# A gelu branch turned round: tokens in partitions, gelu out of PSUM, the result transposed by the matrix engine

## The chip, the cores and the metric

The kernel runs on one core of a Trainium2 chip. The metric is the device time in microseconds of one execution. All data are float32; the large products are computed in split form (below) as float32r matmuls.

## What is computed

Two residual blocks over 256 tokens of width 2048. The change lies in the recurrent branch of the first one:

```
proj = rmsnorm(x) @ w_in                         # xr, yr, q, k, v, g_rnn, g_attn
xr   = rg_lru(causal_conv(xr), ...)              # gates: two block-diagonal products, sigmoid;
                                                 # a = exp(..), h[t] = a[t] h[t-1] + b[t]
y_rnn = xr * gelu(yr)                            # the gelu branch: 2048 features
mix  = sigmoid(g_rnn) * (y_rnn @ w_rnn_proj) + sigmoid(g_attn) * (y_att @ w_attn_proj)
```

An MLP, and then a second block (differential attention and a state-space branch), follow and are not touched.

## The kernel before

**Units.** Every large product is cut into units of 512 output columns with 2048 rows of weights: 16 k tiles, taken in 8 subgroups of two. For a subgroup SyncE loads 512 KB into one of four slots of `raw`; ScalarE rounds them to float32r (`split_hi`, L674, `w_hi`), VectorE subtracts (`split_lo`, L1187, `w_lo`); the matrix engine computes three products, hi*hi, hi*lo and lo*hi. `split_hi` of a subgroup waits until the matrix engine has finished the subgroup four before it (`pe_used`), and the two splitting engines work three subgroups ahead (`LEAD`). Units alternate between the accumulators `acc[0]` and `acc[1]` (two PSUM banks each); `acc_free` tells that one has been read.

**Two forms.** A *token* unit has the activations as the stationary operand (128 tokens) and 512 columns of weights streaming: 2 x 3 matmuls of 512 columns per k tile, 96 in a unit; tokens come out in partitions. A *feature* unit (`by_feature=True`) has 128x128 blocks of weights stationary and 256 tokens streaming: 4 x 3 matmuls of 256 columns per k tile, 192 in a unit; features come out in partitions, as the recurrence along the tokens needs them.

**Order.** Each engine's order is written out by hand: `unit(...)` on the matrix engine and `steps(...)` on ScalarE and VectorE take tables of hooks, called after a given k tile or subgroup. The stage in question: after four pairs of q and xr units (with the attention beside them) come the four units of the gelu branch (U_YR + c, c = 0 to 3), all feature units, then the mix units (token units). The first unit of the branch has the last heads' attention beside it. Beside unit U_YR + c + 1 (for c = 3 beside the first mix unit) runs the recurrence of the 512 features of chunk c:

- the matrix engine, after k tile 1: `rg(c)`, 32 float32 matmuls (L2138); the first gate goes into `tps` (two banks), the second into `sides` (two banks)
- ScalarE: step 0 `gelu(c)` (L865), step 1 `gates(c)` (tanh out of `tps` and `sides`, L838 and L841), step 2 `decays(c)` (L851, L855), step 4 `root(c)` (L860), step 7 `y_high(c)` (L829)
- VectorE: step 3 `decay(c)` (L1451 to L1453), step 5 `states(c)` with the four scans (L1459 to L1466), step 6 `y_product(c)` (L1472), step 7 `y_low(c)` (L1477). For c = 3 the scans are at step 6, the product at step 7 and `y_low` in the next unit.

Each step begins with a split, and the hooks come after it. When a gelu unit is complete, VectorE multiplies it by the row of 1/rms (`L1491`) out of the accumulator into `k_t` or `stg`, in turn; ScalarE puts the gelu over it in place.

Names: `stg`, `tmp`, `tmp2`, `k_t` are 128x1024 buffers in SBUF; `rec4` is `tmp`, `a4` is `tmp2` (the profile may show both as `tmp`), `r4` and `i4` lie in `slab_g` (shown as `slab_dg_f`). `rstd` holds 1/rms of a token by partition, `row` the same along the free dimension. `y_ready` counts two per chunk: scans, product.

Of the kernel before, what the change touches and what calls it, by code (L numbers as in the profile page):

```python
# [16 lines left out]
P = 128  # L17
# [78 lines left out]
def griffin_block_then_ssm_block(nc, a, inv_freq, out):  # L96
    with ExitStack() as ctx:
# [12 lines left out]
        def sem(name):  # L110
            return ctx.enter_context(nc.semaphore(name))
# [98 lines left out]
        conv_ready, rg_done, w_ready = sem("conv_ready"), sem("rg_done"), sem("w_ready")  # L210
        xc_read, tap_ready = sem("xc_read"), sem("tap_ready")
        d_ready, root_ready, y_ready = sem("d_ready"), sem("root_ready"), sem("y_ready")
        y_hi_ready, gelu_ready = sem("y_hi_ready"), sem("gelu_ready")

        z_ready, tanh_ready, zs_ready = sem("z_ready"), sem("tanh_ready"), sem("zs_ready")

# [139 lines left out]
        r4, i4 = slab_g[:, 8:12, :], slab_g[:, 12:16, :]  # L356
        xc4 = stg[:, :, :].rearrange("p t (k c) -> p (t k) c", c=SEQ)
        xr_c = i4
        yr_c = [k_t[:, :, :], xc4]
        turned4 = xc4  # L360
        rec4 = tmp[:, :, :].rearrange("p t (k c) -> p (t k) c", c=SEQ)
        a4 = tmp2[:, :, :].rearrange("p t (k c) -> p (t k) c", c=SEQ)
# [252 lines left out]
        def tok(bank):  # L615
            return bank[:, :].rearrange("p (t n) -> p t n", t=TT)

        def feat(bank):
            return bank[:, :].rearrange("p (k c) -> p k c", c=SEQ)
# [42 lines left out]
        def _(act):  # L662
# [168 lines left out]
            def gates(c):  # L831
                act.wait_ge(rg_done, c + 1)
                if c:
                    act.wait_ge(y_ready, 2 * c)
                else:
                    act.wait_ge(conv_ready, NH + 1)
                for m in range(QPC):
                    nc.scalar.activation(r4[:, m, :], tps[:, m * SEQ:(m + 1) * SEQ], ACT.Tanh, scale=0.5,  # L838
                                         bias=half_b[:, c * QPC + m:c * QPC + m + 1])
                for m in range(QPC):  # L840
                    ins = nc.scalar.activation(i4[:, m, :], side[m // 2][:, m % 2 * SEQ:(m % 2 + 1) * SEQ], ACT.Tanh,  # L841
                                               scale=0.5, bias=half_b[:, KT + c * QPC + m:KT + c * QPC + m + 1])
                chain.mark(ins)

            def decays(c):

                chain.wait()
                act.wait_ge(lam_ready, 1)
                for m in range(QPC):
                    s2 = lru[:, 6, c * QPC + m:c * QPC + m + 1]  # L850
                    ins = nc.scalar.activation(rec4[:, m, :], r4[:, m, :], ACT.Exp, scale=s2, bias=s2)  # L851
                chain.link(ins)
                for m in range(QPC):
                    s2 = lru[:, 7, c * QPC + m:c * QPC + m + 1]
                    ins = nc.scalar.activation(r4[:, m, :], r4[:, m, :], ACT.Tanh, scale=s2, bias=s2)  # L855
                ins.then_inc(w_ready, 1)
# [4 lines left out]

            def gelu(c):
                u = U_YR + c
                act.wait_ge(acc_free[u % 2], u // 2 + 1)
                nc.scalar.activation(yr_c[c % 2], yr_c[c % 2], ACT.Gelu_apprx_tanh).then_inc(gelu_ready, 1)  # L865

            def beside_recurrence(c):
                places = {0: [lambda: gelu(c)], 1: [lambda: gates(c)], 2: [lambda: decays(c)], 4: [lambda: root(c)]}
# [312 lines left out]
        def _(dve):  # L1181
# [16 lines left out]
            def unit_over(i, stride, const):  # L1198
                dve.wait_ge(pe_used, lin(i, stride, const + S))
# [267 lines left out]
                ins.then_inc(y_ready, 1)  # L1467

            def y_product(c):
                dve.wait_ge(gelu_ready, c + 1)  # L1470
                dve.wait_ge(y_ready, 2 * c + 1)
                V.tensor_tensor(a4, yr_c[c % 2], rec4, ALU.mult).then_inc(y_ready, 1)  # L1472

            def y_low(c):
                at = slice(c * QPC, (c + 1) * QPC)
# [8 lines left out]
            for c in range(NH):  # L1484
                u = U_YR + c
                steps(None, 0, u * S, beside_recurrence(c - 1) if c else beside_yr)
                if c == 0:
                    dve.wait_ge(tps_free, T_QX + NH)
                unit_over(None, 0, u * S)
                rows_ = row[:, :].unsqueeze(1).broadcast_to([P, QPC, SEQ])  # L1490
                V.tensor_tensor(yr_c[c % 2], feat(acc[u % 2]), rows_, ALU.mult).then_inc(acc_free[u % 2], 1)  # L1491


            def mix_unit(i, c, n, hooks=None):
# [456 lines left out]
        def _(pe):  # L1951
            T = nc.tensor

            def unit(i, g_stride, g0, u_stride, u, hi, lo, by_feature=False, hooks=None, before=None, k_tiles=KT,
                     halves=False):


                par = u % 2
                hooks, before = hooks or {}, before or {}
                if i is not None or u >= 2:  # L1960
                    pe.wait_ge(acc_free[par], lin(i, u_stride // 2, u // 2))
                for s in range(k_tiles // 2):
                    for f in before.get(s, []):
                        f()
                    pe.wait_ge(lo_ready, lin(i, g_stride, g0 + s + 1))
                    if halves and s == k_tiles // 2 - 1:

                        for t in range(TT):
                            o = acc[par][:, t * NC:(t + 1) * NC]
                            c = slice(t * P, (t + 1) * P)  # L1970
                            for e in range(2):
                                wh, wl = w_hi[:, s % RING, e, :], w_lo[:, s % RING, e, :]
                                T.matmul(o, hi[:, 2 * s + e, c], wh, start=False, stop=False)
                                T.matmul(o, hi[:, 2 * s + e, c], wl, start=False, stop=False)
                                ins = T.matmul(o, lo[:, 2 * s + e, c], wh, start=False, stop=e == 1)
                            ins.then_inc((acc_half, pe_used)[t], 1)
                        break
                    for e in range(2):
                        k = 2 * s + e
                        first, last = k == 0, k == k_tiles - 1  # L1980
                        wh, wl = w_hi[:, s % RING, e, :], w_lo[:, s % RING, e, :]
                        if by_feature:
                            for m in range(QPC):
                                o = acc[par][:, m * SEQ:(m + 1) * SEQ]
                                c = slice(m * P, (m + 1) * P)

                                T.matmul(o, wh[:, c], hi[:, k, :], start=first and m % 2 == 0, stop=False,  # L1987
                                         skip_group_check=True)
                                T.matmul(o, wh[:, c], lo[:, k, :], start=False, stop=False, skip_group_check=True)  # L1989
                                ins = T.matmul(o, wl[:, c], hi[:, k, :], start=False, stop=last, skip_group_check=True)  # L1990
                        else:
                            for t in range(TT):
                                o = acc[par][:, t * NC:(t + 1) * NC]
                                c = slice(t * P, (t + 1) * P)
                                T.matmul(o, hi[:, k, c], wh, start=first, stop=False)  # L1995
                                T.matmul(o, hi[:, k, c], wl, start=False, stop=False)  # L1996
                                ins = T.matmul(o, lo[:, k, c], wh, start=False, stop=last)  # L1997
                        if e == 1:
                            ins.then_inc(pe_used, 1)
                        for f in hooks.get(k, []):  # L2000
                            f()
# [124 lines left out]
            def rg(c):  # L2126
                pe.wait_ge(conv_ready, c + 2)
                pe.wait_ge(rgw_landed[c % 2], 64 * (c // 2 + 1))
                if c:
                    pe.wait_ge(w_ready, c)  # L2130
                else:
                    pe.wait_ge(att_out, 4 * NH)
                for g in range(2):
                    for b in range(2):
                        bank = tps[:, b * NC:(b + 1) * NC] if g == 0 else side[b][:, :]
                        for m in range(2):
                            for k in range(2):
                                ins = T.matmul(bank[:, m * SEQ:(m + 1) * SEQ],  # L2138
                                               rgw[c % 2][g][:, 2 * b + k, m * P:(m + 1) * P], slab_d[:, c * QPC + 2 * b + k, :],
                                               start=k == 0, stop=k == 1)  # L2140
                ins.then_inc(rg_done, 1)

            for c in range(NH):
                unit(None, 0, (U_YR + c) * S, 0, U_YR + c, h_hi, h_lo, by_feature=True,
                     hooks={1: [lambda: rg(c - 1)]} if c else beside_yr)

            def mix_unit(i, c, n, hooks=None):
                hi, lo = ((h_hi, h_lo), (slab_er, slab_ir), (h_hi, h_lo), (slab_fr, slab_hr))[n]
                u = U_MIX + 4 * c + n
                unit(i, 4 * S, u * S, 4, u, hi, lo, hooks=hooks)  # L2150

            mix_unit(None, 0, 0, {1: [lambda: rg(NH - 1)]})
            for c in range(NH - 1):
                for n in (1, 2, 3):
                    mix_unit(None, c, n)
# [197 lines left out]
```

## Time and profile before

| | |
|---|---|
| median of 3 runs | 2240.53 us (2240.46 to 2240.6) |
| profiled execution, its time | 2240.62 us |
| its span, first to last instruction | 2238.9 us |
| matrix engine (PE) busy | 2227.7 us, 99% |
| VectorE (DVE), ScalarE (ACT), GpSimd (POOL) busy | 70%, 54%, 12% |
| mean granted clock of the matrix engine | 1.000 |

The span and what lies around it make up the execution's time (1.7 us more). Matmuls overlap in the pipeline, so the busy share is that of a queue that is never empty and not of a peak rate; the distance from one start to the next is what a matmul costs. PEld are the weight loads. Idle time of an engine stands in brackets, with what ended it.

### The profile page before, as it was taken

The numbers are of one execution on the slowest core, as the hardware profiler recorded it, in microseconds if no ns is written. First come the engines' busy times: TensorE is split into PE (matmuls) and PEld (weight loads), VectorE is DVE, ScalarE is ACT, GpSimd is POOL, SyncE is SP. The second block draws the span as 40 slices with busy tenths as digits, with TensorE's granted clock in tenths as the row PEclk, the third lists the DMA queues.
The fourth block names the chain that finished last, engine by engine and source line by source line (L and its number), as shares of the span: only waits on it lengthen the run. The fifth ranks groups of instructions, "written<-read, shape, count | busy, mean of one in ns | idle before, by whom it ended". The sixth has DMA issues, their size and how long they took to land.

```text
span 2238.9 us, 32782 instructions
## 1 busy us (share of the span) xinstructions
PE 2227.7 (99%) x11645; PEld 1875.1 (84%) x11645; DVE 1575.0 (70%) x2081; ACT 1218.3 (54%) x1915; POOL 275.1 (12%) x319
## 2 busy tenths in 40 slices
PE   9999999999999999999999999999999999999999
PEld 7888999888888888888888888889987788888887
DVE  6666657664664778757857856966999967766774
ACT  6666667544444456555655656555444446554443
POOL 2132220000000102211212121120000001110000
PEclk9999999999999999999999999999999999999999
DMA  8555454666666856666666666665666655555665
GB/s 242 153 170 150 144 186 142 191 194 194 193 189 197 255 189 213 206 208 190 219 206 193 215 209 204 192 219 177 185 185 206 194 179 168 168 161 177 199 200 167
DMA packets 215350, 427.09 MB, mean 191 GB/s; under 512 B 14097, under 2 KB 14385, under 8 KB 214961
## 3 DMA queue, kind: packets, MB, share of 16 engines
q1 hardware_dynamic: 206960, 398.57, 57.3%
q0 software_dynamic: 8048, 26.62, 3.9%
q8 instruction: 91, 1.49, 0.3%
q14 instruction: 43, 0.34, 0.0%
q10 hardware_dynamic: 208, 0.07, 0.0%
HBM read 414.71 MB, written 10.49 MB: 190 GB/s over the span
## 4 chain that ended last, share of the span: by engine, by line
PE 93%; DVE 3%; ACT 2%; issue 1%; DMA 0%; POOL 0%; DVEq 0%; ACTq 0%
PE acc L1995 26%; PE acc L1997 26%; PE acc L1996 26%; PE acc L1987 4%; PE acc L1989 3%; PE acc L1990 3%; PE sides L2213 1%; PE tps L2223 1%; PE sides L2087 1%; PE tps L2105 1%; DVE w_lo L1187 1%; ACT w_hi L674 1%; PE tps L2098 0%; ACT tmp L851 0%; DVE tmp L1466 0%
## 5 line engine op out<-in xcount | busy, mean ns | idle before, releaser
L1187 DVE TENSOR_TENSOR w_lo<-raw,w_hi 128x1024 fp32r<-128x1024 f32 x752 | 927.4, 1243 | 574.1 <-ACT w_hi L674 568.7
L674 ACT ACTIVATE w_hi<-raw 128x1024 fp32r<-128x1024 f32 x752 | 790.3, 1058 | 729.1 <-PE acc L1997 598.1
L1995 PE MATMUL acc<-w_hi,h_hi 128*128 128x512 f32 x1440 | 569.5, 395 | 2.7 <-DVE w_lo L1187 1.8
L1997 PE MATMUL acc<-w_hi,h_lo 128*128 128x512 f32 x1440 | 561.1, 390 | 0.0
L1996 PE MATMUL acc<-w_lo,h_hi 128*128 128x512 f32 x1440 | 560.7, 389 | 0.0
L1995 PEld LDWEIGHTS acc<-w_hi,h_hi 128*128 128x128 f32 x1440 | 270.4, 188 | 69.4 <-issue 15.1
L1997 PEld LDWEIGHTS acc<-w_hi,h_lo 128*128 128x128 f32 x1440 | 270.3, 188 | 57.2
L1996 PEld LDWEIGHTS acc<-w_lo,h_hi 128*128 128x128 f32 x1440 | 270.6, 188 | 53.3
L1995 PE MATMUL acc<-w_hi,slab_dg_r 128*128 128x512 f32 x756 | 294.1, 389 | 0.0
L1996 PE MATMUL acc<-w_lo,slab_dg_r 128*128 128x512 f32 x756 | 294.1, 389 | 0.0
L1997 PE MATMUL acc<-w_hi,slab_dg_r 128*128 128x512 f32 x756 | 294.1, 389 | 0.0
L1987 PE MATMUL acc<-h_hi,w_hi 128*128 128x256 f32 x768 | 221.3, 288 | 0.8 <-issue 0.8
L1989 PE MATMUL acc<-h_lo,w_hi 128*128 128x256 f32 x768 | 217.2, 283 | 0.0
L1990 PE MATMUL acc<-h_hi,w_lo 128*128 128x256 f32 x768 | 217.1, 283 | 0.0
L1211 DVE STREAM_TRANSPOSE stg<-tmp 32x256 f32<-32x256 f32 x384 | 167.3, 436 | 5.8
L1997 PEld LDWEIGHTS acc<-w_hi,slab_dg_r 128*128 128x128 f32 x756 | 141.9, 188 | 29.5
L1996 PEld LDWEIGHTS acc<-w_lo,slab_dg_r 128*128 128x128 f32 x756 | 141.9, 188 | 29.4
L1995 PEld LDWEIGHTS acc<-w_hi,slab_dg_r 128*128 128x128 f32 x756 | 141.9, 188 | 29.4
L1987 PEld LDWEIGHTS acc<-h_hi,w_hi 128*128 128x128 f32 x768 | 146.8, 191 | 7.1 <-issue 6.9
L1989 PEld LDWEIGHTS acc<-h_lo,w_hi 128*128 128x128 f32 x768 | 147.0, 191 | 0.2
L1990 PEld LDWEIGHTS acc<-h_hi,w_lo 128*128 128x128 f32 x768 | 146.9, 191 | 0.0
L1995 PE MATMUL acc<-w_hi,slab_f_r 128*128 128x512 f32 x256 | 100.4, 392 | 0.0
(390 smaller groups left out, 2320.4 us busy)
## 6 DMA issues: line engine op xcount, KB each, us to landing
raw<-in_w_in_dram SPq DMA_DIRECT2D x328, 512.0 KB, 4.0
raw<-in_w_mlp_up_dram SPq DMA_DIRECT2D x128, 512.0 KB, 4.2
raw<-in_w_mlp_down_dram SPq DMA_DIRECT2D x128, 512.0 KB, 4.4
raw<-in_w_out_dram SPq DMA_DIRECT2D x64, 512.0 KB, 4.4
raw<-in_w_rnn_proj_dram SPq DMA_DIRECT2D x32, 512.0 KB, 4.0
raw<-in_w_attn_proj_dram SPq DMA_DIRECT2D x32, 512.0 KB, 4.1
trig_scratch<-tmp POOLq DMA_DIRECT2D x32, 256.0 KB, 4.8
raw<-in_w_proj_ssm_dram SPq DMA_DIRECT2D x16, 512.0 KB, 3.8
```

The costliest lines, as they stand in the source:

```text
L674: nc.scalar.activation(w_hi[:, j % RING], raw[:, j % RING], ACT.Copy).then_inc(hi_ready, 1)
L1187: V.tensor_tensor(w_lo[:, j % RING], raw[:, j % RING], w_hi[:, j % RING].bitcast(F32), ALU.subtract)\
L1211: ins = V.transpose(dst, src)
L1987: T.matmul(o, wh[:, c], hi[:, k, :], start=first and m % 2 == 0, stop=False, skip_group_check=True)
L1989: T.matmul(o, wh[:, c], lo[:, k, :], start=False, stop=False, skip_group_check=True)
L1990: ins = T.matmul(o, wl[:, c], hi[:, k, :], start=False, stop=last, skip_group_check=True)
L1995: T.matmul(o, hi[:, k, c], wh, start=first, stop=False)
L1996: T.matmul(o, hi[:, k, c], wl, start=False, stop=False)
L1997: ins = T.matmul(o, lo[:, k, c], wh, start=False, stop=last)
L2087: ins = T.matmul(side[n][:, t * P:t * P + (t + 1) * P], q_c[at, p, t * P:(t + 1) * P], k_c[at, 0:(t + 1) * P], start=True, stop=True)
L2105: ins = T.matmul(y_banks[64 * n:64 * n + 64, t, :], v_c[:, s, :], prob_t[p % 2][:, n, b * P:(b + 1) * P], start=s == 0, stop=s == t)
L2213: ins = T.matmul(side[j % 2][:, part * SEQ:(part + 1) * SEQ], b_t[at, part, :], u_feat[at, n // 4, :], start=True, stop=True)
```

## The change

The four units of the gelu branch become token units. When one is complete, ScalarE takes the gelu directly out of the accumulator, with 1/rms as the scale per partition, in two activations of 128x512 into `stg`. VectorE's multiplication goes. The matrix engine then turns the eight 128x128 blocks of `stg` into `tps`, after k tile 7 of the next unit (`turn_yr`), once `gates` has read both gates there; the product takes its operand from `tps`. The next `rg` writes `tps` too, so it now waits for that product (`y_ready` at 2c) and for `gates_read`, where it waited for `w_ready`. Two semaphores take the place of `gelu_ready` and of a link of ScalarE's chain.

```diff
--- before.py
+++ after.py
@@ -210,7 +210,8 @@
         conv_ready, rg_done, w_ready = sem("conv_ready"), sem("rg_done"), sem("w_ready")
         xc_read, tap_ready = sem("xc_read"), sem("tap_ready")
         d_ready, root_ready, y_ready = sem("d_ready"), sem("root_ready"), sem("y_ready")
-        y_hi_ready, gelu_ready = sem("y_hi_ready"), sem("gelu_ready")
+        y_hi_ready = sem("y_hi_ready")
+        gates_read, yr_turned = sem("gates_read"), sem("yr_turned")
 
         z_ready, tanh_ready, zs_ready = sem("z_ready"), sem("tanh_ready"), sem("zs_ready")
 
@@ -356,7 +357,6 @@
         r4, i4 = slab_g[:, 8:12, :], slab_g[:, 12:16, :]
         xc4 = stg[:, :, :].rearrange("p t (k c) -> p (t k) c", c=SEQ)
         xr_c = i4
-        yr_c = [k_t[:, :, :], xc4]
         turned4 = xc4
         rec4 = tmp[:, :, :].rearrange("p t (k c) -> p (t k) c", c=SEQ)
         a4 = tmp2[:, :, :].rearrange("p t (k c) -> p (t k) c", c=SEQ)
@@ -840,11 +840,11 @@
                 for m in range(QPC):
                     ins = nc.scalar.activation(i4[:, m, :], side[m // 2][:, m % 2 * SEQ:(m % 2 + 1) * SEQ], ACT.Tanh,
                                                scale=0.5, bias=half_b[:, KT + c * QPC + m:KT + c * QPC + m + 1])
-                chain.mark(ins)
+                ins.then_inc(gates_read, 1)
 
             def decays(c):
 
-                chain.wait()
+                act.wait_ge(gates_read, c + 1)
                 act.wait_ge(lam_ready, 1)
                 for m in range(QPC):
                     s2 = lru[:, 6, c * QPC + m:c * QPC + m + 1]
@@ -861,8 +861,14 @@
 
             def gelu(c):
                 u = U_YR + c
-                act.wait_ge(acc_free[u % 2], u // 2 + 1)
-                nc.scalar.activation(yr_c[c % 2], yr_c[c % 2], ACT.Gelu_apprx_tanh).then_inc(gelu_ready, 1)
+                unit_over(None, 0, u * S)
+                if c:
+                    act.wait_ge(yr_turned, c)
+                else:
+                    act.wait_ge(tps_ready, T_QX + NH)
+                for t in range(TT):
+                    ins = nc.scalar.activation(stg[:, t, :], tok(acc[u % 2])[:, t, :], ACT.Gelu_apprx_tanh, scale=rstd[:, t:t + 1])
+                ins.then_inc(acc_free[u % 2], 1)
 
             def beside_recurrence(c):
                 places = {0: [lambda: gelu(c)], 1: [lambda: gates(c)], 2: [lambda: decays(c)], 4: [lambda: root(c)]}
@@ -1467,9 +1473,9 @@
                 ins.then_inc(y_ready, 1)
 
             def y_product(c):
-                dve.wait_ge(gelu_ready, c + 1)
+                dve.wait_ge(yr_turned, c + 1)
                 dve.wait_ge(y_ready, 2 * c + 1)
-                V.tensor_tensor(a4, yr_c[c % 2], rec4, ALU.mult).then_inc(y_ready, 1)
+                V.tensor_tensor(a4, feat(tps), rec4, ALU.mult).then_inc(y_ready, 1)
 
             def y_low(c):
                 at = slice(c * QPC, (c + 1) * QPC)
@@ -1484,11 +1490,6 @@
             for c in range(NH):
                 u = U_YR + c
                 steps(None, 0, u * S, beside_recurrence(c - 1) if c else beside_yr)
-                if c == 0:
-                    dve.wait_ge(tps_free, T_QX + NH)
-                unit_over(None, 0, u * S)
-                rows_ = row[:, :].unsqueeze(1).broadcast_to([P, QPC, SEQ])
-                V.tensor_tensor(yr_c[c % 2], feat(acc[u % 2]), rows_, ALU.mult).then_inc(acc_free[u % 2], 1)
 
 
             def mix_unit(i, c, n, hooks=None):
@@ -2127,7 +2128,8 @@
                 pe.wait_ge(conv_ready, c + 2)
                 pe.wait_ge(rgw_landed[c % 2], 64 * (c // 2 + 1))
                 if c:
-                    pe.wait_ge(w_ready, c)
+                    pe.wait_ge(gates_read, c)
+                    pe.wait_ge(y_ready, 2 * c)
                 else:
                     pe.wait_ge(att_out, 4 * NH)
                 for g in range(2):
@@ -2140,16 +2142,26 @@
                                                start=k == 0, stop=k == 1)
                 ins.then_inc(rg_done, 1)
 
+            def turn_yr(c):
+                u = U_YR + c
+                pe.wait_ge(acc_free[u % 2], u // 2 + 1)
+                pe.wait_ge(gates_read, c + 1)
+                for t in range(TT):
+                    for b in range(QPC):
+                        ins = T.transpose(tps[:, b * SEQ + t * P:b * SEQ + (t + 1) * P], stg[:, t, b * P:(b + 1) * P],
+                                          ident[:, :])
+                ins.then_inc(yr_turned, 1)
+
             for c in range(NH):
-                unit(None, 0, (U_YR + c) * S, 0, U_YR + c, h_hi, h_lo, by_feature=True,
-                     hooks={1: [lambda: rg(c - 1)]} if c else beside_yr)
+                unit(None, 0, (U_YR + c) * S, 0, U_YR + c, h_hi, h_lo,
+                     hooks={1: [lambda: rg(c - 1)], 7: [lambda: turn_yr(c - 1)]} if c else beside_yr)
 
             def mix_unit(i, c, n, hooks=None):
                 hi, lo = ((h_hi, h_lo), (slab_er, slab_ir), (h_hi, h_lo), (slab_fr, slab_hr))[n]
                 u = U_MIX + 4 * c + n
                 unit(i, 4 * S, u * S, 4, u, hi, lo, hooks=hooks)
 
-            mix_unit(None, 0, 0, {1: [lambda: rg(NH - 1)]})
+            mix_unit(None, 0, 0, {1: [lambda: rg(NH - 1)], 7: [lambda: turn_yr(NH - 1)]})
             for c in range(NH - 1):
                 for n in (1, 2, 3):
                     mix_unit(None, c, n)
```

## Rows read from the trace of the kernel before

**Rows 1.** The page: engines, busy us, share, instructions; granted clock in tenths
```profile
PE 2227.7 (99%) x11645; PEld 1875.1 (84%) x11645; DVE 1575.0 (70%) x2081; ACT 1218.3 (54%) x1915; POOL 275.1 (12%) x319
...
PEclk9999999999999999999999999999999999999999
```

**Rows 2.** Waits of PE over the span: total us, times, longest us
```profile
PE acc L1995 <- DVE w_lo L1187: 1.8, 2, 1.2
```

**Rows 3.** The chain of waits, 170 to 480 us: start us, us, what
```profile
296.02 1.57 ACT slab_dg_f L838 x4
...
400.92 1.15 DVE w_lo L1187
402.11 0.50 PE acc L1995
```

**Rows 4.** Timeline of PE and PEld, gate matmuls: start us, us, instruction
```profile
288.80 0.74 PEld L2138 LDWEIGHTS tps<-slab_dg_f 128*128 128x128 f32 x4
...
295.63 0.47 PE L1987 MATMUL acc<-h_hi,w_hi 128*128 128x256 f32 x1
...
318.74 0.31 PEld L2138 LDWEIGHTS tps<-slab_dg_f,slab_e_f 128*128 128x128 f32 x2
...
348.68 0.31 PEld L2138 LDWEIGHTS tps<-slab_dg_f 128*128 128x128 f32 x2
...
378.38 0.19 PEld L2138 LDWEIGHTS tps<-slab_dg_f,slab_e_f 128*128 128x128 f32 x1
```

**Rows 5.** Timeline of ACT and DVE in the first round
```profile
305.43 1.99 ACT L674 ACTIVATE w_hi<-raw 128x1024 fp32r<-128x1024 f32 x2
...
306.51 1.23 DVE L1187 TENSOR_TENSOR w_lo<-raw,w_hi 128x1024 fp32r<-128x1024 f32 x1 [5.23 <-ACT w_hi L674]
...
313.32 1.22 DVE L1459 SCALAR_TENSOR_TENSOR slab_dg_f<-tmp,slab_dg_f 128x1024 f32<-128x1024 f32 x1
...
319.31 1.22 DVE L1472 TENSOR_TENSOR tmp<-k_t,tmp 128x1024 f32<-128x1024 f32 x1
```

**Rows 6.** Timeline of DVE, the product of the third round
```profile
379.19 1.22 DVE L1472 TENSOR_TENSOR tmp<-k_t,tmp 128x1024 f32<-128x1024 f32 x1
```

**Rows 7.** Timeline of PE, first matmuls of units
```profile
200.43 0.50 PE L1995 MATMUL acc<-w_hi,h_hi 128*128 128x512 f32 x1
...
228.61 0.28 PE L1987 MATMUL acc<-h_hi,w_hi 128*128 128x256 f32 x1
...
256.98 0.38 PE L1987 MATMUL acc<-h_hi,w_hi 128*128 128x256 f32 x1
...
286.03 0.28 PE L1987 MATMUL acc<-h_hi,w_hi 128*128 128x256 f32 x1
...
404.99 0.39 PE L1995 MATMUL acc<-w_hi,slab_e_r 128*128 128x512 f32 x1
...
426.81 0.39 PE L1995 MATMUL acc<-w_hi,h_hi 128*128 128x512 f32 x1
```

**Rows 8.** Timeline of PE, eight transposes inside a token unit
```profile
49.91 1.03 PE L2010 MATMUL tps<-ident,stg 128*128 128x128 f32 x8
50.70 0.48 PE L1995 MATMUL acc<-w_hi,h_hi 128*128 128x512 f32 x1
51.01 0.40 PE L1996 MATMUL acc<-w_lo,h_hi 128*128 128x512 f32 x1
```

**Rows 9.** Timeline of PE, the matmul before the wait at 402 us
```profile
401.61 0.39 PE L1997 MATMUL acc<-w_hi,h_lo 128*128 128x512 f32 x1
```

**Rows 10.** ACT by line, 400 to 470 us; timeline of ACT and DVE
```profile
L894 ACT ACTIVATE tmp<-acc,small 128x512 f32<-128x512 f32 x4 | 2.5, 684 | 1.8 <-PE acc L1997 1.7
...
322.79 1.22 DVE L1491 TENSOR_TENSOR stg<-acc,t_low 128x1024 f32<-128x1024 f32 x1
...
324.05 1.06 ACT L865 ACTIVATE stg<-stg 128x1024 f32<-128x1024 f32 x1 [0.18 <-DVE stg L1491]
...
325.96 1.57 ACT L838 ACTIVATE slab_dg_f<-tps,half_b 128x256 f32<-128x256 f32 x4
```

## The prediction, made before the changed kernel was run

> **What bounds the kernel now.** I read the page first: the matrix engine is busy 99% of the span at the full granted clock (2.4 GHz) in all forty slices [rows 1]. Next the matrix engine's own waits: the longest single one is 1.2 us, and waits for VectorE's `w_lo` come to 1.8 us in all [rows 2]. So a microsecond added to or removed from the matrix engine's queue in this stage moves the end by a microsecond, unless another engine is late there. The chain of waits warns of just that: from the end of the first gate matmuls at 296 us to 402 us it runs through ScalarE and VectorE [rows 3], although the matrix engine waits for neither until the last 0.3 us. Something there must be nearly late, and I looked for it in the timeline.
>
> The loop is this. In each unit after the first of the branch, the matrix engine does one pair of k tiles (a subgroup), then the 32 float32 gate matmuls (L2138), then the other seven subgroups. The gate results go through `gates`, `decays`, `decay`, `root`, `states`, `scans` and end in `y_product`, all placed among the weight splits in the fixed orders of ScalarE and VectorE. The first weight load of the gate matmuls starts at 288.80, 318.74, 348.68 and 378.38 [rows 4]: intervals of 29.94, 29.94 and 29.70, in sum 89.58 us. The product of the first round starts at 319.31 and lasts 1.22: it ends at 320.53, which is **31.73 us after its gate matmuls began** [rows 4, 5]. In round three it is 379.19 + 1.22 - 348.68 = 31.73 again [rows 6]. The product thus ends 1.8 us after the next gate matmuls have begun. Before the change this harms nobody: it reads `k_t` or `stg` and `tmp`, no bank.
>
> **The new wait, the largest term.** After the change `y_product` reads the gelu from `tps`, and `rg(c)` writes `tps` again. So `rg` waits for `y_ready` at 2c, the end of the product of the round before. That end comes 31.73 us after its own round's start, and the queue is in order: everything behind `rg(c)` on the matrix engine stands still. Is the chain to the product paced by the matrix engine, so that it would shrink or stretch with it? The rows say no [rows 3, 5]. `gates` starts at 296.02 when the gate matmuls end, then come a split, `decays`, two splits from 305.43, VectorE's `w_lo` from 306.51, three steps of `decay`, two `w_lo`, `states` from 313.32, `scans`, a `w_lo`, and the product at 319.31. Each begins within a fraction of a microsecond of the one before it (the table loads of ScalarE fill the rest). Those splits that wait for the matrix engine (the tightest is the one between `gates` and `decays`, which wants two subgroups done) find it done at the same point of the round as now, or earlier: one token subgroup takes 2.72 us where a feature subgroup takes 2.88 (both below). I take 31.73 as it is.
>
> Without the wait the matrix engine would be back at `rg` after: gate matmuls 6.83 (288.80 to 295.63, [rows 4]); 84 matmuls of the seven subgroups; the eight transposes; 12 matmuls of the next first subgroup. An undisturbed token unit goes from 404.99 to 426.81, 21.82 us for 96 matmuls [rows 7], 0.227 each. So 84 are 19.1, plus 0.2 for the change of data type; 12 are 2.7. The transposes: 49.91 to 50.70 is 0.79 for the same eight blocks from `stg` to `tps`, and the first matmul behind it holds the next one up until 51.01, 0.31 where 0.23 is usual: 0.87 in all [rows 8]. Sum 29.7. The product ends at 31.73: a stall of 2.0 to 2.1 us.
>
> A start after a wait: VectorE's split at 400.92 ends at 402.07, the matrix engine starts at 402.11 [rows 3], so 0.04; and the first matmul there is put at 0.50 against 0.39 [rows 3, 9], since its weight load is not hidden. I take 0.04 + 0.08, between nothing and 0.3 as the bounds. A round is then 31.85. Three rounds are held (`rg(1)`, `rg(2)`, `rg(3)`): 3 x 31.85 = 95.55 against 89.58, **+6.0 us** (bounds: 5.6 with nothing, 6.5 with 0.3 each).
>
> **The first unit of the branch** has attention beside it. The same hooks ran beside a token unit from 200.43 to 228.61, 28.18 us; the feature unit took 256.98 to 286.03, 29.05 us [rows 7]. Saved 0.87, and 0.16 on the first subgroup of the next unit, before `rg(0)`: **-1.0**. The saving of the other three units (192 matmuls at 0.120, 23.1 us from 295.63 to 318.74 [rows 4], against 21.8: 1.3 each) goes into the stall and is in the 31.85 already. So do the three sets of transposes.
>
> What has the Trainium skill on this? The row shows 0.120 us a matmul of 256 columns and 0.227 of 512, a saving of 1.3 us a unit. "TensorE: Matmul & The Clock Gate", section "Back-to-back issue gap", gives N/2.4 + 2.5 ns, so by it, as an estimate, 109 and 216 ns and only 0.24 us a unit; it speaks against half of what turning the operands round could win. By that figure the first unit saves 0.2, not 0.9, and the sum would be 0.8 higher. The rows decide.
>
> **After `rg(3)`.** The fourth turn stands in the first mix unit, in nobody's shadow: +0.87. In exchange the wait for `w_lo` there goes (the matmul before it began at 401.61, so the next was due at 401.84 and began at 402.11, [rows 3, 9]): the matrix engine, 0.87 later, finds it ready; 0.27 of pause and 0.11 of restart are saved, 0.38. Together **+0.5**. The product of round three and `tanh` behind it keep their distance from `rg(3)`; the matrix engine comes 0.5 later to them, so nothing new is late.
>
> **What costs nothing.** `L1491` (1.22 us of VectorE, four times [rows 10]) goes. It stands after the product, and VectorE's next splits are for subgroups that the matrix engine wants only after 6.8 us of gate matmuls. The gelu becomes two activations from the bank, by the nearest row 684 ns each for one of 1.06 us: 0.3 us more on ScalarE. After the product ScalarE does `y_high`, a split, the table load, the gelu, a split, and then `gates`: the second round's `gates` begins at 325.96, 5.4 us after the product's end, a wait of 0.18 for L1491 included [rows 10]. With 0.3 more that is 5.7, while the gate matmuls will end 7 us after the product. Cover 1.3 us; if it were gone each microsecond would lengthen the round by one. `turn_yr` waits for the gelu and `gates_read`: `gates` is done 10.2 us after the round starts, the turn comes at 15. The product's other operand in a bank: L1491 read a bank and took 1.22 as well. `acc_free` comes from ScalarE about when it came from VectorE, and the bank is wanted a unit later. No transfer is issued or moved.
>
> **Sum.** -1.0 + 6.0 + 0.5 = +5.4 us on the profiled execution's 2240.62, hence 2246.0; its time is 0.1 above the median of the runs, which changes nothing that I can forecast. Behind the first mix unit all is bound by the matrix engine, so nothing is given back.
>
> **Rivals.**
> *The product is in time (not slower).* If the round's chain were under 29.7 us, no stall: -1.0 in the first part, 3 x (-1.3 + 0.87) = -1.3, +0.5 after: -1.8, 2238.8. For it: VectorE is without L1491. Against: L1491 is behind the product, not ahead of it, and both rounds show 31.73. It decides from 2.0 us off the chain. A chain shorter by 1 us leaves 2243.
> *The round grows.* The longer stall lets ScalarE's queue slip into `gates`: if the gelu cost the table load twice (1.28) or the split before it were late, rounds of 33: 3 x 33 - 89.6 = +9.4, and 2249.5. Against: 1.3 us of cover.
> *The clock falls in the stall.* A pause of 2 us is longer than any in the profile (1.2). At 1.2 GHz the gate matmuls after it take 6.8 more: +20, 2266. Against: the pauses at the start left the granted clock full [rows 1]. The same page of the Trainium skill, section Part 1, "The HAM clock gate", has the throttled state as the default that activity lifts; here no row shows it.
> *Faster.* It would take no stall and transposes at nothing: -1.0 - 3.9 - 0.4 = -5.3, 2235.3. The transposes take 0.79 in the queue wherever they stand.
>
> **Numbers.** Stall as worked out 0.70 (its own range 2245.0 to 2247.3), in time 0.10, shorter chain with part of the stall 0.08, grown round 0.08, clock 0.02, faster 0.02. A change under 0.2% (4.5 us, up to 2245.0) can't be told from none. Slower: 0.70 less the part of it that may fall short, plus 0.10, 0.75; faster 0.02; same 0.23. The range from 2242.0 to 2248.5 leaves out the case without a stall and most of the grown rounds.
>
> **What would show it.** Matrix engine idle about 2 us ahead of the gate matmuls three times, released by VectorE's product; gate matmuls 31.8 us apart; no idle ahead of the fourth turn; nothing waiting at 402; from the second mix unit on the old pattern, 5.4 later. Wrong if the product ends sooner than 31.5 after its gate matmuls, or if `gates` starts late.

## The result and the profile after

The changed kernel takes **2250.86 us** (median of 6 runs, 2248.79 to 2252.55) against 2240.49 us for the kernel before (6 runs): ratio 1.0046, 95% interval 1.0036 to 1.0056. It is slower, as forecast, but by 10.4 us where 5.4 were forecast, and outside the stated range (up to 2248.5). Its runs also spread over 3.8 us, those of before over 1.0.

The page of the changed kernel, engines and granted clock, beside [rows 1]:

```profile
span 2248.9 us, 32088 instructions
## 1 busy us (share of the span) xinstructions
PE 2231.7 (99%) x11293; PEld 1860.7 (83%) x11293; DVE 1569.6 (70%) x2077; ACT 1219.7 (54%) x1919; POOL 274.9 (12%) x319
...
PEclk9999999999999999999999999999999999999999
```

It shows next to nothing: the matrix engine is busy 99% as before, and the clock reads 9 in every slice. The only hint is the mean granted clock that goes with the run, 0.998 for 1.000; over a span of 2249 us, 0.002 short is 4 to 5 us. Five of the six runs have 0.998 and the slowest has 0.997. The waits of the matrix engine have a new first row, beside [rows 2]:

```profile
PE tps L2140 <- DVE tmp L1478: 6.0, 3, 2.0
```

L2140 are the gate matmuls, L1478 is the product: three pauses of 2.0 us. The timeline of the weight loads there, beside [rows 4]; the four starts are 31.94, 33.50 and 31.82 us apart where they were 29.94, 29.94 and 29.70:

```profile
286.93 0.19 PEld L2140 LDWEIGHTS tps<-slab_dg_f 128*128 128x128 f32 x1
...
318.87 0.30 PEld L2140 LDWEIGHTS tps<-slab_dg_f,slab_e_f 128*128 128x128 f32 x2 [2.40 <-issue]
...
352.37 0.30 PEld L2140 LDWEIGHTS tps<-slab_dg_f 128*128 128x128 f32 x2 [2.35 <-issue]
...
384.19 0.30 PEld L2140 LDWEIGHTS tps<-slab_dg_f,slab_e_f 128*128 128x128 f32 x2 [2.39 <-issue]
```

One interval is 1.6 us longer than its neighbours, though the pause ahead of it is no longer. The matmuls tell why:

```profile
302.24 1.03 PE L2151 MATMUL tps<-ident,stg 128*128 128x128 f32 x8
303.03 0.48 PE L1996 MATMUL acc<-w_hi,h_hi 128*128 128x512 f32 x1
...
318.90 5.38 PE L2140 MATMUL tps<-slab_dg_f,slab_e_f 128*128 128x256 f32 x16 [2.00 <-DVE tmp L1478]
...
352.40 3.69 PE L2140 MATMUL tps<-slab_dg_f 128*128 128x256 f32 x16 [1.96 <-DVE tmp L1478]
...
384.22 5.38 PE L2140 MATMUL tps<-slab_dg_f,slab_e_f 128*128 128x256 f32 x16 [2.00 <-DVE tmp L1478]
```

The same 16 matmuls take 3.69 us in one round and 5.38 in the two others. The stretches (window and its length in us, then busy time and instructions of each engine, then the granted clock as a share of 2.4 GHz, DMA):

```profile
316.70:318.90 2.20, 0.20 (x2) 0.03 (x1) 2.20 (x3) 0.12 (x1) 0.00 (x0) 1.00 0.07 11
...
320.30:323.70 3.40, 3.40 (x10) 2.65 (x9) 1.94 (x2) 3.37 (x5) 0.00 (x0) 0.50 0.78 227
...
350.40:352.40 2.00, 0.04 (x2) 0.03 (x1) 2.00 (x3) 0.12 (x1) 0.00 (x0) 1.00 0.03 9
352.40:359.20 6.80, 6.80 (x33) 6.00 (x33) 4.56 (x4) 5.38 (x6) 0.00 (x0) 1.00 0.77 228
...
385.10:388.50 3.40, 3.40 (x10) 2.73 (x9) 2.46 (x3) 3.37 (x5) 0.00 (x0) 0.50 0.83 264
832.30:835.70 3.40, 3.40 (x9) 2.62 (x9) 2.81 (x6) 2.08 (x5) 0.00 (x0) 0.50 0.00 0
```

Behind two of the three pauses the clock stands at 0.50, 1.2 GHz, for 3.4 us, and the matrix engine does half the work in them: 1.7 us lost each time. A third such stretch is at 832 us, where the turning of x for the MLP (transposes of the normalised x on the matrix engine) makes two pauses of 0.67 and 0.77 us. The first of the two is longer than in the kernel before:

```profile
821.79 1.36 PE L2032 MATMUL tps<-ident,slab_i_f 128*128 128x128 f32 x8 [0.30 <-DVE slab_i_f L1613]
...
829.99 1.36 PE L2033 MATMUL tps<-ident,slab_i_f 128*128 128x128 f32 x8 [0.67 <-DVE slab_i_f L1614]
```

(the first line from the kernel before, the second from the changed one). Forty slices of 56 us hide all three falls.

So the books of the profiled execution (2250.59 against 2240.62, +9.97) are: the first unit and all ahead of `rg(0)` 286.93 - 288.80 = -1.9, of which 0.7 is a start of the program that was 0.7 us quicker; the three rounds (384.19 - 286.93) - 89.58 = +7.7; from `rg(3)` to the second mix unit 28.69 for 26.61, +2.1; behind it +2.1, of which 1.7 is the fall at 832 and 0.37 the longer pause there. Three falls make 5.1 of the 10.0.

### The profile page after: what moved, and what is told of

Its sections match the earlier page's. It is cut to its first block, busy times and chain, and to the rows that moved or that the text cites. A ratio compares the mean times of both kernels' runs of the same rounds, so it can differ in the third digit from the quotient of the medians.

```text
span 2248.9 us, 32088 instructions
## 1 busy us (share of the span) xinstructions
PE 2231.7 (99%) x11293; PEld 1860.7 (83%) x11293; DVE 1569.6 (70%) x2077; ACT 1219.7 (54%) x1919; POOL 274.9 (12%) x319
## 4 chain that ended last, share of the span: by engine, by line
PE 95%; DVE 2%; ACT 2%; issue 1%; DMA 0%; POOL 0%; DVEq 0%; ACTq 0%
PE acc L1996 27%; PE acc L1998 26%; PE acc L1997 26%; PE acc L1988 3%; PE acc L1990 3%; PE acc L1991 3%; PE tps L2140 1%; PE sides L2225 1%; PE tps L2235 1%; PE sides L2140 1%; PE sides L2088 1%; PE tps L2106 1%; PE tps L2099 0%; ACT w_hi L674 0%; DVE w_lo L1193 0%
## 5 line engine op out<-in xcount | busy, mean ns | idle before, releaser
L1996 PE MATMUL acc<-w_hi,h_hi 128*128 128x512 f32 x1568 | 621.6, 396 | 2.0 <-DVE w_lo L1193 1.2
L1998 PE MATMUL acc<-w_hi,h_lo 128*128 128x512 f32 x1568 | 611.8, 390 | 0.0
L1997 PE MATMUL acc<-w_lo,h_hi 128*128 128x512 f32 x1568 | 611.3, 390 | 0.0
L1996 PEld LDWEIGHTS acc<-w_hi,h_hi 128*128 128x128 f32 x1568 | 294.8, 188 | 74.0 <-issue 15.6
L1988 PE MATMUL acc<-h_hi,w_hi 128*128 128x256 f32 x512 | 147.5, 288 | 0.8 <-issue 0.8
L1990 PE MATMUL acc<-h_lo,w_hi 128*128 128x256 f32 x512 | 144.8, 283 | 0.0
L1991 PE MATMUL acc<-h_hi,w_lo 128*128 128x256 f32 x512 | 144.7, 283 | 0.0
L1988 PEld LDWEIGHTS acc<-h_hi,w_hi 128*128 128x128 f32 x512 | 97.8, 191 | 5.9 <-issue 5.7
L1998 PE MATMUL acc<-w_hi,slab_h_r 128*128 128x512 f32 x256 | 99.7, 389 | 0.0
L1997 PE MATMUL acc<-w_lo,slab_f_r 128*128 128x512 f32 x256 | 99.6, 389 | 0.0
```

## The experiments

**Theory A:** the pause costs its length as forecast, and besides it lets the granted clock fall, which is the missing half. **Theory B:** the missing half comes from the new order itself (product from the bank, token units, later stages). **Theory C**, for the second set: pauses matter, but only among the changed kernel's instructions. Times are medians, each beside the kernel before on the same chip.

| kernel | us | before | ratio (95%) | pauses, us | low clock in the stage (profile) |
|---|---|---|---|---|---|
| changed | 2250.86 | 2240.49 | 1.0046 (1.0036 to 1.0056) | 2.00, 1.96, 2.00 | 2 of 3 |
| fill | 2246.14 | 2240.82 | 1.0026 (1.0016 to 1.0035) | none | none |
| fill_part | 2245.76 | 2241.08 | 1.0021 (1.0012 to 1.0031) | 1.36, 1.32, 1.31 | none |
| wait_alone | 2246.86 | 2240.82 | 1.0027 (1.0016 to 1.0038) | 1.66, 1.66, 1.79 | none |
| product_early | 2243.19 | 2240.82 | 1.0011 (1.0002 to 1.0020) | 1.09, 1.01, 1.08 | none |
| later_product | 2255.05 | 2241.08 | 1.0063 (1.0049 to 1.0077) | 3.14, 3.08, 3.11 | 3 of 3 |
| later_wait | 2256.37 | 2241.08 | 1.0068 (1.0054 to 1.0081) | 2.80, 2.79, 2.92 | 3 of 3 |
| copy_out | 2240.58 | 2240.82 | 0.9997 (0.9988 to 1.0006) | none | none |
| copy_and_warm | 2239.74 | 2241.08 | 0.9995 (0.9986 to 1.0004) | none | none |
| before_filled | 2240.85 | 2240.80 | 1.0000 (0.9991 to 1.0009) | none | none |
| copy_filled | 2239.82 | 2240.80 | 0.9996 (0.9987 to 1.0005) | none | none |

### fill: work in place of the pause

```diff
                 if c:
                     pe.wait_ge(gates_read, c)
+                    keep_turning(20)
                     pe.wait_ge(y_ready, 2 * c)
```

> The changed kernel with 20 transposes of the identity (into the second bank pair of the gates, which nobody reads any more) put ahead of the wait for the product, so that the matrix engine works through the pause instead of standing still. The three pauses stay as long, only filled. Theory A (the pause costs its own length, and twice a fall of the granted clock besides): the gate matmuls start 31.8 us apart all three times, the clock stays at 2.4 GHz in this stage, and the time is that of the forecast, 2245 to 2247. Theory B (the extra 5 us come from the new order itself: the operand in a bank, the token units, the later stages): nothing changes or it gets slower, 2249 to 2252.

2246.14, and the rounds are 31.9, 31.8 and 31.8 us. The stretches of fill around the three starts of the gate matmuls, at the full clock and without a gap:

```profile
318.00:330.00 12.00, 12.00 (x66) 10.64 (x65) 6.49 (x6) 8.43 (x15) 2.67 (x4) 1.00 0.63 184
350.00:362.00 12.00, 12.00 (x65) 10.58 (x64) 6.26 (x6) 8.65 (x15) 0.00 (x0) 1.00 0.63 177
382.00:394.00 12.00, 12.00 (x64) 10.54 (x63) 6.03 (x6) 8.83 (x15) 0.00 (x0) 1.00 0.59 176
```

More instructions, the product comes no sooner, and 4.7 us are gone. Theory B falls: product, token units and later stages are all as in the changed kernel. What remains, 5.3 us, is the forecast's 5.4.

### wait_alone: only the wait, in the kernel before

```diff
                 if c:
                     pe.wait_ge(w_ready, c)
+                    pe.wait_ge(y_ready, 2 * c)
```

> The kernel before with one line more: rg(c) also waits for the product of the round before. Nothing else of the change. The matrix engine would be back after 29.9 us, the product ends at 31.73, so each of three rounds grows by 1.9 us: +5.7, 2246.2, by the wait alone. Theory A: the clock falls here too after some of these pauses of 1.9 us, each fall up to 1.7 us, so 2246 to 2251, with the falls visible as windows of lower granted clock behind the pauses. Theory B: the full clock and 2246.2.

2246.86, +6.0 for the +5.7 worked out. The waits of wait_alone and the stretches behind them:

```profile
PE tps L2139 <- DVE tmp L1472: 5.1, 3, 1.8
...
318.00:330.00 12.00, 10.34 (x61) 9.34 (x60) 8.02 (x7) 7.78 (x12) 2.22 (x4) 1.00 0.56 167
350.00:362.00 12.00, 10.34 (x61) 9.34 (x60) 7.86 (x7) 7.95 (x13) 0.00 (x0) 1.00 0.60 168
```

The wait alone, without anything else of the change, costs about what the changed kernel loses at full clock (5.3 in fill). But no clock falls here, behind pauses of 1.7 to 1.8 us; theory A had left that open. Is it the length (2.0 against 1.7) or the surroundings? fill_part and later_wait ask that.

### copy_out: the change without its wait

```diff
+            def yr_copy(c):
+                act.wait_ge(yr_turned, c + 1)
+                if c:
+                    act.wait_ge(y_ready, 2 * c)
+                nc.scalar.activation(k_t[:, :, :], feat(tps), ACT.Copy).then_inc(yr_copied, 1)
...
+                          6: [lambda: yr_copy(c)]}
...
-                dve.wait_ge(yr_turned, c + 1)
+                dve.wait_ge(yr_copied, c + 1)
...
-                V.tensor_tensor(a4, feat(tps), rec4, ALU.mult).then_inc(y_ready, 1)
+                V.tensor_tensor(a4, k_t[:, :, :], rec4, ALU.mult).then_inc(y_ready, 1)
...
-                    pe.wait_ge(gates_read, c)
-                    pe.wait_ge(y_ready, 2 * c)
+                    pe.wait_ge(yr_copied, c)
```

> The changed kernel with the turned gelu copied by ScalarE out of the banks into k_t at step 6 (1.06 us, where ScalarE has time), the product from k_t as before, and rg(c) waiting for that copy and no longer for the product. Token units, gelu out of the accumulator and transposes stay. Theory A: no pause, no fall of the clock; -1.0 before the first gates, 3 x (0.87 - 1.3) in the rounds, +0.5 behind: 2238.7, between 2237 and 2240, faster than both kernels. Theory B: a good part of the 10 us stays, 2243 or more.

2240.58, 10 us below the changed kernel, for one activation more in each round. The weight loads of the gate matmuls in copy_out, 29.57, 29.61 and 29.68 us apart (29.7 was worked out without a wait), and the copy, which lies among ScalarE's splits:

```profile
287.32 0.19 PEld L2147 LDWEIGHTS tps<-slab_dg_f 128*128 128x128 f32 x1
...
316.89 0.19 PEld L2147 LDWEIGHTS tps<-slab_dg_f,slab_e_f 128*128 128x128 f32 x1
...
346.50 0.19 PEld L2147 LDWEIGHTS tps<-slab_dg_f 128*128 128x128 f32 x1
...
376.18 0.19 PEld L2147 LDWEIGHTS tps<-slab_dg_f,slab_e_f 128*128 128x128 f32 x1
...
310.37 1.00 ACT L878 ACTIVATE k_t<-tps 128x1024 f32<-128x1024 f32 x1
```

That is the whole 10 us, but not the 2238.7 expected: it ties with the kernel before. Of the 1.8 us that should be won, the profile shows 1.1 up to the second mix unit (256.66 to 403.60 us, where before took 256.98 to 404.99). By the starts of the gate matmuls the first unit gives -1.0 and the three rounds -0.8 for the -1.3 expected; behind `rg(3)` it is +0.8 for +0.5, because the matrix engine waits for `w_lo` again (matmuls at 400.34 and 400.75). Then the longer pause at the turning of x takes 0.36 back. Its profile, of one of the slower runs, has a stretch of low clock besides, with the two pauses ahead of it:

```profile
820.81 1.36 PE L2041 MATMUL tps<-ident,slab_i_f 128*128 128x128 f32 x8 [0.66 <-DVE slab_i_f L1622]
822.93 0.47 PE L2004 MATMUL acc<-w_hi,h_hi 128*128 128x512 f32 x1 [0.77 <-issue]
...
823.30:826.70 3.40, 3.40 (x10) 2.62 (x9) 2.63 (x5) 1.91 (x5) 0.00 (x0) 0.51 0.00 0
```

### product_early: a shorter pause

```diff
-                ... 5: [lambda: states(c)], 6: [lambda: y_product(c)], 7: [lambda: y_low(c)]}
+                ... 5: [lambda: states(c), lambda: y_product(c)], 7: [lambda: y_low(c)]}
```

> The changed kernel with y_product one split earlier on VectorE (behind the scans, ahead of the split of step 6). The chain from the gate matmuls to the product becomes 1.1 us shorter, the pause about 1.0 us in place of 2.1. At full clock: 3 x 30.7 - 89.6 = +2.5, in all -1.0 + 2.5 + 0.5 = +2.0: 2242.5. Theory A with a clock that falls only after long enough a pause: 2242 to 2243 and the full clock; if pauses of 1 us are enough for a fall, 2244 to 2248. Theory B: about 3 us below the changed kernel, 2247 to 2248, with the full clock or without.

2243.19, full clock, pauses of 1.0 to 1.1 us, rounds of 31.0, 30.9 and 30.9 for the 30.7 expected. A product one split earlier takes 1 us off each pause, and 7.7 us off the whole: 3 us of pauses, and the falls behind them.

### fill_part: a part of the pause filled

```diff
+                    keep_turning(5)
```

(where fill has 20.)

> As fill, but with 5 transposes in place of 20: they cover some 0.5 us of each 2.0 us pause, and 1.5 us of idle time stay, in the same place and before the same instructions. The rounds stay 31.8 us long. If the length of the pause decides on the clock (theory A), the clock stays full as with the 1.7 us pauses of wait_alone, and the time is 2246 to 2247. If it is the token units or the operand in the bank that lets the clock fall once the matrix engine stands still at all (theory C), the clock falls again: 2249 to 2252.

2245.76; the waits of fill_part and one of its stretches:

```profile
PE tps L2141 <- DVE tmp L1478: 4.0, 3, 1.4
...
317.00:329.00 12.00, 10.64 (x51) 9.04 (x50) 6.66 (x6) 8.28 (x14) 2.52 (x4) 1.00 0.58 177
```

The changed kernel's own surroundings, with pauses of 1.3 to 1.4 us, keep the full clock, so its units and its operand in the bank don't make the clock fall at any pause. Whether a pause needs these surroundings to bring a fall at all is for later_wait to say. Five transposes, 0.5 us, are worth as much as twenty.

### later_product and later_wait: longer pauses in either kernel

```diff
-                ... 6: [lambda: y_product(c)], 7: [lambda: y_low(c)]}
+                ... 7: [lambda: y_product(c), lambda: y_low(c)]}
```

(later_product is the changed kernel with this, later_wait is wait_alone with this.)

> The changed kernel with y_product behind the split of step 7, one split later: the chain grows by 1.1 us to 32.9, the pause to 3.2 us. The order is kept, only the wait is longer. At full clock 3 x 33.0 - 89.6 = +9.4, with -1.0 and +0.5 in all +8.9: 2249.7. Theory A: the clock falls behind each of the three pauses, 1.7 us each, 2253 to 2255, and falls in all three rounds. If the clock is a matter of chance and not of the length, falls in one or two: 2251 to 2253.

> The kernel before with the wait alone (as wait_alone) and y_product one split later: feature units, gelu in SBUF, no transposes, but a pause of about 2.9 us. At full clock 3 x 33.0 - 89.6 = +9.4: 2250.2. Theory A: length decides, so the clock falls here too, up to 3 x 1.7 more, 2252 to 2255. Theory C (only the changed kernel's units are exposed): full clock, 2250.2.

The stretches of later_product, pauses included:

```profile
317.00:329.00 12.00, 8.86 (x35) 7.23 (x33) 6.93 (x6) 5.50 (x6) 0.00 (x0) 0.86 0.48 138
352.00:364.00 12.00, 8.93 (x34) 7.55 (x34) 6.57 (x6) 5.50 (x6) 0.00 (x0) 0.86 0.49 143
387.00:399.00 12.00, 9.22 (x35) 7.82 (x36) 6.21 (x6) 5.85 (x7) 0.00 (x0) 0.86 0.50 155
```

and of later_wait:

```profile
318.00:330.00 12.00, 9.20 (x40) 7.82 (x40) 7.83 (x7) 5.46 (x6) 0.00 (x0) 0.86 0.47 139
352.00:364.00 12.00, 9.21 (x32) 7.56 (x32) 8.18 (x8) 5.29 (x5) 0.00 (x0) 0.72 0.46 137
388.00:400.00 12.00, 9.08 (x35) 7.33 (x33) 8.12 (x8) 5.29 (x5) 0.00 (x0) 0.86 0.45 134
```

0.86 over 12 us is 1.7 us lost, 0.72 is 3.4, of which 0.4 falls into the pause itself. All six pauses bring a fall, in feature units as in token units, so theory C falls too. later_product: 2249.7 by the pauses plus 3 x 1.7 gives 2254.8, measured 2255.05. later_wait came out at 2256.37, above the expected 2252 to 2255: one of its falls lasted twice as long as I had reckoned.

### copy_and_warm, before_filled, copy_filled: the version without the wait, against its control

```diff
-        WARM = [26, 32]
+        WARM = [33, 37]
```

> copy_out with more filler transposes at the two places where the kernel already has them, ahead of the turning of x for the MLP and for the second block (33 and 37 in place of 26 and 32), which should cover the idle 0.66 and 0.50 us there. copy_out has two levels, 2239.5 and 2241.2, and its profile shows one fall of the clock at 823 us, behind two pauses of 0.66 and 0.77 us. If that fall makes the upper level, the upper level goes: 2239.3 to 2239.8 throughout. If not, the two levels stay, or the fillers cost 0.1 to 0.2 us each.

> The kernel before with the fillers of copy_and_warm alone (33 and 37). It separates the two parts of copy_and_warm, 1.3 us below the kernel before. If the fillers make it (a fall of the clock at 824 us in some executions, and 0.5 us of pause that has a price only then), this is 2240.0 to 2240.4 where before is 2241, and copy_and_warm, run beside it, at most 0.5 lower. If the turned units without the wait are worth the 1.0 us that their stage shows, copy_and_warm is 0.8 to 1.2 us below this kernel.

> The kernel of copy_and_warm again, on the same chip as before_filled. See there: 0.8 to 1.2 us below it if the turned units are worth their stage's gain, 0 to 0.5 if not. Against the kernel before: 0.9993 to 0.9996.

copy_and_warm: 2239.74 (2238.97 to 2240.75), its profile at the full clock in the stretch of the MLP's start. before_filled: 2240.85, as the kernel before, so the fillers alone gain nothing there; copy_filled on the same chip: 2239.82, 1.0 us lower. That is the worth of the turned units, and it agrees with their stage (-1.1 in copy_out, above). The intervals against the kernel before (0.9995 and 0.9996) include 1, so it is a best version by medians and not beyond the measurement.

Where the upper runs of copy_out come from can be read from the mean granted clock, which is on record for every run: one stretch of 3.4 us at 0.50 in 2240 us makes it 0.999, two or three make it 0.998, four 0.997. The four slowest of its 11 runs (2241.1 to 2241.6) have 0.999, the seven others (2239.4 to 2240.8) 1.000. So the upper level is one fall each, and the profile of one of the four has it at 823 us. The kernels whose pause at the turning of x is 0.30 us (before, wait_alone) or filled (before_filled, copy_and_warm, copy_filled) have 1.000 in all of their 112 runs. Those with the 0.66 or 0.67 us of the token units and no longer pause than 1.4 us elsewhere (copy_out, fill, fill_part, product_early) have 0.999 in 10 of 43. That points to the longer pause; only copy_out has a profile of such a run.

## Why the prediction was half right

- **The new wait.** Right. The product ends 31.8 us after its gate matmuls began (317.54 + 1.21 - 286.93, a round of before 31.73); pauses of 2.0, 2.0 and 2.0 us for 2.0 to 2.1 forecast; three rounds of 31.8 to 31.9 where the clock stays full, as in fill. The operand in the bank costs nothing: 1.21 us.

```profile
317.54 1.21 DVE L1478 TENSOR_TENSOR tmp<-tps,tmp 128x1024 f32<-128x1024 f32 x1
```

- **The first unit.** Right: from its first matmul at 256.27 to the first of the gates at 287.16, 30.89 us for 31.93 before, -1.04 (forecast -1.03).
- **After `rg(3)`.** Right but for the clock: 28.69 - 26.61 = 2.08, less 1.7 for the fall is 0.4 (forecast 0.5). Nothing waits at 402 any more; the transposes take the 0.79 us of [rows 8]. Not right is "nothing is given back" behind the first mix unit: the pause at the turning of x grew from 0.30 to 0.67 us, in every profiled kernel whose branch is in token units (but for those with more fillers there) and in none with feature units. The runs don't tell why.
- **What costs nothing.** Right, with more cover than worked out: the two activations of the gelu take 1.27 us, and `gates` waits 3.45 us for the matrix engine in this (slowed) round; less the 1.7 of the fall some 1.7 us of cover are left, for 1.3 forecast.

```profile
322.10 1.27 ACT L870 ACTIVATE stg<-acc,small 128x512 f32<-128x512 f32 x2
323.26 1.06 ACT L674 ACTIVATE w_hi<-raw 128x1024 fp32r<-128x1024 f32 x1
327.77 1.57 ACT L838 ACTIVATE slab_dg_f<-tps,half_b 128x256 f32<-128x256 f32 x4 [3.45 <-PE sides L2140]
```

- **The step that failed: "The clock falls in the stall".** The sum has no term for the clock. The fall was written down as a rival at a chance of 2%, since "the pauses at the start left the granted clock full". What the runs show in its place: in the profile two of the three 2.0 us pauses bring a stretch of 3.4 us at half clock, at 1.7 us each, and a third fall follows at 832 us. The reason given against it was misread. The longest wait in the view of [rows 2] is not 1.2 us but 1.7, ahead of the program's very first matmul, and the clock was not full then. These are transposes of the same 128x128 identity, at the start and at 818 us of the kernel before:

```profile
1.66 2.40 PE L2017 MATMUL sides<-ident 128*128 128x128 f32 x10 [1.66 <-POOL ident L464]
...
818.50 3.00 PE L2017 MATMUL sides<-ident 128*128 128x128 f32 x26
```

0.24 us each against 0.12: the engine starts at half its speed, as at 1.2 GHz, though the profile's clock reads full there too. That this is the clock is argued from the spacing; no row states it. The pauses between matmuls at full speed were 1.2 us at most; I had the longer one in the same sentence (2 us, longer than any in the profile) and gave it no weight. The rival was mis-sized too: 6.8 us for each, as if all the gate matmuls ran at 1.2 GHz, where a fall lasts 3.4 us and costs 1.7. With two or three falls and the forecast's 5.4, the sum is 2249.4 to 2251.1, where the median of the changed kernel lies. The Trainium skill ("TensorE: Matmul & The Clock Gate", Part 1, "The HAM clock gate") has low clock as the default state, which activity lifts. The trace agrees, with the slow transposes at the start and the clock at 0.50 behind two of the pauses of 2.0 us.
- **The sum.** -1.0 + 6.0 + 0.5 stands: fill, the changed kernel with the matrix engine kept at work, took 2246.14 where the forecast was 2246.0. The measured kernel is that plus falls. The 0.37 us of the longer pause is too little to show in the medians.

**What stays open.** It isn't told why one of three equal pauses of 2.0 us was spared. By their mean granted clocks five of the six runs of the changed kernel (0.998) have two or three falls and the slowest (0.997) has four; which pauses brought them is recorded for one run alone. Nor is it told why the pause at the turning of x is followed by a fall in some executions and not in others: six profiled kernels have it at 0.66 or 0.67 us, and two of them, the changed kernel and copy_out, fell there.

## What to carry to other kernels

When a result is handed over in a bank that the next round writes again, compare two lengths before anything else: from the writer's start to the reader's end, and from one start of the writer to the next. The first was 31.7 us, the second 29.7, and no saving elsewhere in the round can help; a copy out of the bank by an engine with time to spare (1.0 us) took the whole loss away. And price a pause of the matrix engine twice, once at its length and, from the lengths on at which falls were seen (here 2.0 us), once for the clock behind it. If it can't be removed, some filler matmuls in it were worth 4.7 us here.

## What the runs showed of the hardware

- Pauses of the matrix engine within this dense stage, in the profiles: six of 1.3 to 1.8 us, and three of 1.0 to 1.1, without a fall; three of 2.0 us, two with a fall; six of 2.8 to 3.1 us, all with a fall. In the low stretches the granted clock is 0.50 and each fall costs 1.7 us, once 3.4.
- Two pauses of 0.66 or 0.67 and 0.77 us, 2.1 us apart, were followed by a fall in two of six profiles: 0.51 at 823 us in copy_out, 0.50 at 832 us in the changed kernel. With 0.30 and 0.77 us none of three fell.
- The matrix engine begins the program at half speed: 0.24 us for a transpose of 128x128 at 1.7 us, 0.12 at 818 us.
- The page doesn't show any of it: the clock's tenths read 9 throughout. The mean granted clock of the run (0.998) and a table of stretches do; at the start of the program neither does, and the spacing of like matmuls must.
- Turned the other way, a unit takes 21.8 us for 23.1: 0.227 us for 512 columns, 0.120 for 256. The transposes take 0.87 of the 1.3 back, so the turned form is worth 0.4 us a unit by this sum. In the whole kernel it is worth 1.0 us once nothing waits for the product, and that is the first unit's: what the rounds gain, the stretch behind `rg(3)` loses.
